# Modulation pieces in four column groups, and layer 0's first two pieces turned into columns on TensorE

## The chip, the cores and the metric

One Trainium2 chip, one core. The metric is the device time of one launch in microseconds (us), the median of several runs. TensorE multiplies (a stationary operand is loaded, a moving one streams past it), VectorE and ScalarE work element by element, GpSimd does the rest, SyncE issues most DMAs. All data are float32; each float32 matmul of the program is two records (two passes) in the trace, a transpose is one.

## The reference

Two layers of a transformer over 1024 tokens of an image and 256 of context, 1024 wide. Each layer is modulated: six vectors of 1024 numbers, for each of two conditions, are made from the conditions and shift, scale and gate what the layer does. Layer 0 mixes by retention and neighbourhood attention, layer 1 by windowed attention, and both go on with a mixture of 32 experts.

```python
s_c, s_cc = silu(c), silu(c_ctx)
for layer in range(2):
    sh1, sc1, g1, sh2, sc2, g2 = split((s_c @ ada_w[layer] + ada_b[layer])[:, None, :], 6)
    csh1, csc1, ... = split((s_cc @ ada_w[layer] + ada_b[layer])[None, None, :], 6)
    hx = rms_norm(x, norm_g[layer, 0]) * (1 + sc1) + sh1
    hc = rms_norm(xc, norm_g[layer, 0]) * (1 + csc1) + csh1
    ox, oc = mixer(hx, hc)
    x = x + g1 * ox;  xc = xc + cg1 * oc
    h2 = rms_norm(x, norm_g[layer, 1]) * (1 + sc2) + sh2
    x = x + g2 * moe(h2)          # likewise xc in layer 0
out = rms_norm(x, final_g)
```

ada_w is 2 x 1024 x 6144 in float32, 50 MB in all.

## The kernel before

The modulation is cut into 12 **pieces**: piece s is vector j = s % 6 of layer l = s // 6, 1024 columns of ada_w, for both conditions. Each piece has 4 MB of weights in two halves of 512 columns, loaded by `ada_load` (two DMAs of 2 MB) into one of two buffer pairs, and from piece 6 on into one pair alone (`ada_ring`), so that load s + 1 waits there for product s. `ada_product` multiplies on TensorE: the stationary operand is a 128 x 2 slice of the activated conditions (`sT`, one column for each condition), the moving one 512 columns of weights; half h writes partitions 32h and 32h + 1 of one PSUM bank, that is, column group h of the array, accumulating over eight slices k. `ada_evict` on VectorE adds the biases (which `ada_rows` has loaded into the row buffer `modrow[s % 2]`), and for the scale vectors (j of 1 and 4) computes (1 + scale) times the norm's gain. `ada_out` writes the two rows to the memory tensor `mod`. Later stages read gates and shifts from there as rows.

The first shift and scale of a layer (pieces 0, 1 and 6, 7) are wanted as columns, feature 8p + k of a vector in partition p: `ada_cols` reads them back from `mod` into `colab`. In layer 0 ScalarE issues these writes and reads (`ada_out(act, 0)`, `ada_out(act, 1)`, `ada_cols(act, 0)` in `n1_act`), in layer 1 SyncE.

The stage around them: `n1_act` and `n1_dve` compute each tile's root mean square and normalise it, `n1_pe` transposes it on TensorE (`turn`), and both engines evict the transposed tile to `hT` with `colab` as scale and bias. Behind that runs the projection `pa`: 40 **units**, each eight matmuls of 128 x 128 by 512 for one tile and one chunk of 512 columns of weights; before unit i, TensorE transposes tile i + 1, waits for tile i's eviction, and for odd i below 20 runs product 2 + i // 2. So TensorE's order is: products 0 and 1, transposes of tiles 0 and 1, unit 0, transposes of tile 2, product 2, unit 1, and so on until product 11. Products 0 and 1 run ahead of all, and their pieces are evicted between the scale computations of the decay (`ada_dve`) and after the normalising of tiles 0 and 1 (`n1_dve`).

SyncE's queue is written out by hand in `ada_sp`: loads of pieces 0 and 1 with their biases, three tiles of x, the first chunk of projection weights, then load 2, tiles, biases of piece 2, load 3, biases of piece 3, and so on. From piece 6 on the order is: write of piece s, biases of piece s + 2, load of piece s + 2. The biases of piece s + 2 go into the row buffer of piece s, so they wait until its write to memory has landed.

Semaphores are shared between names that follow one another: `share` maps a name to an earlier one, and `done` adds the earlier total.

## Time and profile before

| what | value |
| --- | --- |
| median of 3 runs | 2951.45 us (2949.23 to 2952.83) |
| profiled execution | 2954.52 us |
| its span, first to last instruction | 2952.4 us |
| TensorE matmul busy | 2734.9 us (93%), 11488 matmuls |
| VectorE busy | 1003.3 us (34%) |
| ScalarE busy | 594.2 us (20%) |
| GpSimd busy | 253.8 us (9%) |
| mean granted TensorE clock | 0.961 |
| moved by DMA | 602.72 MB, mean 204 GB/s |

The profile comes from one execution. Times in the trace count from the span's start. PE is TensorE's matmul side and PEld its weight loads, which overlap; DVE is VectorE, ACT ScalarE, SPq and ACTq the DMA issuing of SyncE and ScalarE. In a row of the timeline the first number is the start, the second the length of the merged group, and the brackets say how long the engine idled before it and what released it. Matmuls are pipelined, so that a record's length is not its price; the distance between starts is.

### The profile page before, as it was taken

Reading aid. Unit: us, or ns where it says so; the run is one execution under the profiler, and the core shown is the slowest. Engines: PE = TensorE matmul, PEld = TensorE weight load, DVE = VectorE, ACT = ScalarE, POOL = GpSimd, SP = SyncE. Lnnn points to the kernel's source line nnn. Section 1 sums busy time; section 2 is a strip of 40 time slices with the busy share of each in tenths; the row PEclk is TensorE's granted clock in tenths of the full one; section 3 lists DMA queues with packets and bytes.
Section 4 is the critical chain, followed back from the end, with each engine's and each line's share of the span. In section 5 each row is a group of like instructions: output and inputs, shape, how many; then the busy total and the mean of one; then the engine's idle time right before and its main releaser. Section 6 shows DMA issues by size and latency. Waiting matters only on the chain. (4 is left out here: it accounts for less than half of the span.)

```text
span 2952.4 us, 30072 instructions
## 1 busy us (share of the span) xinstructions
PE 2734.9 (93%) x11488; PEld 1401.9 (47%) x11488; DVE 1003.3 (34%) x2373; ACT 594.2 (20%) x1187; POOL 253.8 (9%) x359
## 2 busy tenths in 40 slices
PE   5999999999989799999999779989999799999991
PEld 1434446555745444444444334467765444444440
DVE  2221227306736621111111074267746511111113
ACT  2201101116821100000000041068831100000002
POOL 0011020003011100000000000000011100000003
PEclk8999999999999899999999989999999799999995
DMA  8654110205050289999999540030030599999994
GB/s 315 229 198 146 27 38 26 75 0 112 2 221 31 92 316 331 365 389 333 383 362 339 216 174 29 0 64 2 2 124 36 205 386 403 404 405 403 401 395 186
DMA packets 225944, 602.72 MB, mean 204 GB/s; under 512 B 18056, under 2 KB 21136, under 8 KB 217224
## 3 DMA queue, kind: packets, MB, share of 16 engines
q1 hardware_dynamic: 209976, 545.15, 51.2%
q0 software_dynamic: 15264, 55.58, 4.8%
q8 instruction: 94, 1.54, 0.2%
q14 instruction: 50, 0.41, 0.0%
q10 hardware_dynamic: 560, 0.03, 0.0%
HBM read 556.57 MB, written 44.42 MB: 204 GB/s over the span
## 5 line engine op out<-in xcount | busy, mean ns | idle before, releaser
L1688 PE MATMUL PS<-ar 128*128 128x512 f32 x2016 | 883.8, 596 | 3.4 <-DVE ar L1886 2.6
L778 PE MATMUL PS<-ar 128*128 128x512 f32 (+1 forms) x1600 | 678.5, 580 | 16.1 <-ACT ar L579 14.9
L1688 PEld LDWEIGHTS PS<-ar 128*128 128x128 f32 x2016 | 379.8, 191 | 475.4 <-issue 470.9
L778 PEld LDWEIGHTS PS<-ar 128*128 128x128 f32 x1600 | 300.3, 191 | 354.5 <-issue 334.9
L1308 PE MATMUL PS<-ar 128*128 128x512 f32 x576 | 255.9, 598 | 0.6 <-DVEq L331 0.6
L1691 PE MATMUL PS<-ar 128*64 128x512 f32 x1056 | 238.8, 605 | 15.4 <-DMA ar<-in_expert_w_gu_dram 13.7
L1182 DVE CUSTOM_DVE_ANT_0 ar<-PS,ar 128x640 f32<-128x640 f32 (+2 forms) x208 | 158.1, 797 | 204.7 <-POOL ar L1098 133.5
L1899 DVE COPY ar<-PS 128x512 f32<-128x512 f32 x53 | 36.7, 692 | 514.3 <-PE PS L1701 514.3
L1808 ACT ACTIVATE ar<-PS 128x512 f32<-128x512 f32 x53 | 31.7, 597 | 728.5 <-PE PS L1688 538.0
L1308 PEld LDWEIGHTS PS<-ar 128*128 128x128 f32 x576 | 107.6, 191 | 123.7 <-issue 122.9
L1237 ACT ACTIVATE ar<-ar 128x641 f32<-128x641 f32 (+4 forms) x208 | 159.5, 772 | 0.8 <-DVE ar L1182 0.8
L1691 PEld LDWEIGHTS PS<-ar 128*64 128x64 f32 x1056 | 77.6, 139 | 165.5 <-issue 163.4
L1226 ACT ACTIVATE ar<-PS 128x512 f32<-128x512 f32 (+1 forms) x208 | 133.6, 655 | 72.6 <-PE PS L1140 68.4
L1893 DVE TENSOR_TENSOR ar<-PS,ar 128x512 f32<-128x512 f32 x53 | 36.6, 691 | 323.7 <-PE PS L1688 239.6
L1128 PE MATMUL PS<-ar 64*128 64x256 f32 (+1 forms) x800 | 134.1, 453 | 11.7 <-DVE ar L1182 10.4
L1140 PE MATMUL PS<-cst,ar 128*128 128x128 f32 x944 | 128.5, 281 | 1.0 <-DVE ar L1192 0.8
L1151 PE MATMUL PS<-ar 128*64 128x128 f32 x1888 | 125.6, 278 | 0.0
L1140 PEld LDWEIGHTS PS<-cst,ar 128*128 128x128 f32 x944 | 102.6, 142 | 42.0 <-issue 34.7
L1962 POOL DMA_INDIRECT yd<-ar x53 | 51.8, 977 | 792.4 <-ACT ar L1814 417.6
L1814 ACT ACTIVATE ar<-PS 128x1024 f32<-128x1024 f32 x29 | 29.7, 1025 | 414.7 <-PE PS L1688 370.7
L1151 PEld LDWEIGHTS PS<-ar 128*64 128x64 f32 x1888 | 101.0, 136 | 17.2 <-issue 16.6
L489 PE MATMUL PS<-ar 128*2 128x512 f32 x384 | 89.3, 620 | 20.3 <-DMA ar<-in_ada_w_dram 20.3
(226 smaller groups left out, 1966.7 us busy)
## 6 DMA issues: line engine op xcount, KB each, us to landing
ar<-in_expert_w_gu_dram SPq DMA_DIRECT2D x128, 2048.0 KB, 17.7
ar<-in_expert_w_down_dram SPq DMA_DIRECT2D x64, 2048.0 KB, 17.3
ar<-in_ada_w_dram SPq DMA_DIRECT2D x24, 2048.0 KB, 13.5
ar<-yd SPq DMA_DIRECT2D x36, 512.0 KB, 6.7
ar<-in_ab_w_in_dram SPq DMA_DIRECT2D x7, 2048.0 KB, 9.0
h2d<-ar SPq DMA_DIRECT2D x18, 512.0 KB, 2.6
ar<-in_swa_w_in_dram SPq DMA_DIRECT2D x3, 2048.0 KB, 10.6
ar<-mod SPq DMA_DIRECT2D x3, 1536.0 KB, 8.0
```

The lines of the kernel that those rows point to most:

```text
L489: mm = nc.tensor.matmul(PS[32 * h:32 * h + 2, ada_bank(s), :], sT[:, k, :], adaw[q][h][:, k, :], start=(k == 0), stop=(k == KC - 1))
L778: mm = nc.tensor.matmul(out_, lhs, rhs, start=(k == 0), stop=(k == KC - 1))
L1128: mm = nc.tensor.matmul(score_cols(a, half, at, keys.shape[1]), u["q"][rows_], keys[rows_], start=True, stop=True)
L1140: tr = nc.tensor.transpose(turned_cols(to, P), xat[layer][2 * (i % 3) + a][:, c * P:c * P + P], ident)
L1151: mm = nc.tensor.matmul(slot_of(i)[64 * a:64 * a + 64], half["vs"][c], ptb[layer][i % 2][:, turned_at(a, half["n"]) + c * P:][:, 0:P], sta ...
L1182: nc.vector.tensor_tensor_reduce(out=xat[layer][b][:, 0:w], in0=score_cols(a, half, half["segs"][0][1], w), in1=half["bias"], scale=-SCALE ...
L1226: nc.scalar.activation(ptb[layer][i % 2][:, at:at + w], turned_cols(at, w), ACT.Copy).then_inc(S(f"{n}_pt"), 1)
L1237: nc.scalar.activation(x, x, ACT.Exp, bias=amx[:, b:b + 1], scale=-1.0, accum_out=sums[:, b:b + 1]).then_inc(S(f"{n}_e"), 1)
L1308: mm = nc.tensor.matmul(PS[:, 2 + half, :], mixed(i, k), WO[l][:, k, half * 512:half * 512 + 512], start=(k == 0), stop=(k == KC - 1))
L1688: return nc.tensor.matmul(out, lhsT, ws[0][:, k, cols], start=start, stop=stop)
L1691: mm = nc.tensor.matmul(out[half], lhsT[:, half], ws[h][:, k, cols], start=start, stop=stop)
L1962: pool.indirect_dma_start(out=yd, out_offset=bass.IndirectOffsetOnAxis(ap=dst_i[:, c:c + 1], axis=0), in_=yb[b % 2], in_offset=None).then_ ...
```

## The change

- A piece is multiplied in four column groups of 256 columns instead of two of 512: 32 matmuls for each piece instead of 16, in partitions 32c and 32c + 1 for c from 0 to 3. Row buffers have 256 columns in these partitions, and biases, gains and writes are strided over partitions accordingly, two DMAs for each as before (one for each condition).
- `ada_evict` has four instructions of 256 columns for each step instead of two of 512.
- Pieces 0 and 1 are no longer written to `mod` and read back. `ada_turn` on TensorE makes their columns: for each group c and each k, the stationary operand is 2 x 32 (every eighth number of the rows), the moving one 2 x 2 of the identity; the result is 32 partitions of two columns in bank 4 + s. Both turns stand behind product 1 and ahead of the transposes of tiles 0 and 1. Turn 0 waits for piece 0's eviction, turn 1 for the scaled rows of piece 1. `ada_columns` on VectorE copies them to `colab`.
- ScalarE issues none of these DMAs; it and VectorE wait for `cols0` before the first eviction in layer 0.
- The biases of pieces 2 and 3 wait for turns 0 and 1 instead of for writes.
- Three pairs of semaphores are shared that weren't.

```diff
--- before.py
+++ after.py
@@ -299,6 +299,9 @@
         for before, after in (("masks_in", "band_in1"), ("gain_in", "sink_in"), ("cos_in0", "cos_in1"), ("cos_in1", "fg_in")):
             share(("{}",), before, after, 16)
 
+        for before, after in (("dec_ln", "dec_pos"), ("dec_pos", "dec_exp"), ("silu_c", "rpb_scaled")):
+            share(("{}",), before, after, 1)
+
         chains = {}
 
         class Chain:
@@ -340,8 +343,8 @@
 
         ADA = 12
         adaw = [[R(a, 4096).rearrange("p (k n) -> p k n", k=KC) for a in pair] for pair in ((10240, 20480), (25600, 29696))]
-        modrow = [ar[0:34, a:a + 512] for a in (24576, 25088)]
-        ngrow = ar[0:34, 14400:14912]
+        modrow = [ar[:, a:a + 256] for a in (24576, 25088)]
+        ngrow = ar[:, 14400:14656]
         cin = R(14336, 16).rearrange("p (s k) -> p s k", s=2)
         sT = R(14352, 16).rearrange("p (k s) -> p k s", k=KC)
         rpbs = ar[0:NAH, 15360:15360 + 961].rearrange("p (c i) -> p c i", c=31)
@@ -371,35 +374,38 @@
                 sp.dma_start(adaw[q][h], A["ada_w"][l].rearrange("(p k) n -> p k n", k=KC)[:, :, c:c + 512])\
                     .then_inc(S(f"ada_in{q}"), 16)
 
+        def four(row):
+
+            return row.rearrange("(c n) -> c n", c=4)
+
         def ada_rows(sp, s):
 
             l, j = ada_of(s)
-            if s >= 2:
-                sp.wait_ge(*done(f"mod_out{s % 2}", 32 * (s // 2)))
-            for h in range(2):
-                sp.dma_start(modrow[s % 2][32 * h:32 * h + 2], A["ada_b"][l, j * D + h * 512:j * D + h * 512 + 512].partition_broadcast(2))\
-                    .then_inc(S(f"ada_b{s % 2}"), 16)
+            if s in (2, 3):
+                sp.wait_ge(*done("mod_tr", s - 1))
+            elif s > 3:
+                sp.wait_ge(*done(f"mod_out{s % 2}", 32 * (s // 2 - 1)))
+            for q in range(2):
+                sp.dma_start(modrow[s % 2][q:P:32], four(A["ada_b"][l, j * D:j * D + D])).then_inc(S(f"ada_b{s % 2}"), 16)
             if j in (1, 4):
                 if s > 1:
-                    sp.wait_ge(*done("mod_rows", 2 * (2 * l + j // 3)))
-                for h in range(2):
-                    sp.dma_start(ngrow[32 * h:32 * h + 2], A["norm_g"][l, j // 3, h * 512:h * 512 + 512].partition_broadcast(2))\
-                        .then_inc(S("ng_in"), 16)
+                    sp.wait_ge(*done("mod_rows", 4 * (2 * l + j // 3)))
+                for q in range(2):
+                    sp.dma_start(ngrow[q:P:32], four(A["norm_g"][l, j // 3])).then_inc(S("ng_in"), 16)
 
         def ada_out(eng, s):
             l, j = ada_of(s)
             if j in (1, 4):
-                eng.wait_ge(*done("mod_rows", 2 * (2 * l + j // 3 + 1)))
+                eng.wait_ge(*done("mod_rows", 4 * (2 * l + j // 3 + 1)))
             else:
-                eng.wait_ge(*done("ada_ev", 2 * (s + 1)))
-            for h in range(2):
-                c = j * D + h * 512
-                eng.dma_start(mod[l, :, c:c + 512], modrow[s % 2][32 * h:32 * h + 2]).then_inc(S(f"mod_out{s % 2}"), 16)
+                eng.wait_ge(*done("ada_ev", 4 * (s + 1)))
+            for q in range(2):
+                eng.dma_start(four(mod[l, q, j * D:j * D + D]), modrow[s % 2][q:P:32]).then_inc(S(f"mod_out{s % 2}"), 16)
 
         def ada_cols(eng, l):
 
             for q in range(2):
-                eng.wait_ge(*done(f"mod_out{q}", 32 * (3 * l + 1)))
+                eng.wait_ge(*done(f"mod_out{q}", 32 * 3))
             for s in range(2):
                 eng.dma_start(colab[:, l, s], mod[l, s, 0:2 * D].rearrange("(j p k) -> p j k", j=2, k=KC))\
                     .then_inc(S("cols_in"), 16)
@@ -483,30 +489,52 @@
             q = ada_ring(s)
             pe.wait_ge(*done(f"ada_in{q}", 32 * ada_fills(s)))
             if s >= 2:
-                pe.wait_ge(*done("ada_ev", 2 * (s - 1)))
+                pe.wait_ge(*done("ada_ev", 4 * (s - 1)))
             for k in range(KC):
-                for h in range(2):
-                    mm = nc.tensor.matmul(PS[32 * h:32 * h + 2, ada_bank(s), :], sT[:, k, :], adaw[q][h][:, k, :],
-                                          start=(k == 0), stop=(k == KC - 1))
+                for c in range(4):
+                    mm = nc.tensor.matmul(PS[32 * c:32 * c + 2, ada_bank(s), 0:256], sT[:, k, :],
+                                          adaw[q][c // 2][:, k, (c % 2) * 256:(c % 2) * 256 + 256], start=(k == 0), stop=(k == KC - 1))
             mm.then_inc(S("ada_mm"), 1)
+
+        def ada_turn(pe, s):
+
+            if s == 0:
+                pe.wait_ge(*done("consts", 32))
+                pe.wait_ge(*done("ada_ev", 4))
+            else:
+                pe.wait_ge(*done("mod_rows", 4))
+            for c in range(4):
+                at = slice(32 * c, 32 * c + 2)
+                for k in range(KC):
+                    tr = nc.tensor.matmul(PS[32 * c:32 * c + 32, 4 + s, 2 * k:2 * k + 2],
+                                          modrow[s][at].rearrange("s (p k) -> s k p", k=KC)[:, k, :], cst[at, C_ID + 32 * c:C_ID + 32 * c + 2],
+                                          start=True, stop=True)
+            tr.then_inc(S("mod_tr"), 1)
 
         def ada_pe(pe):
             pe.wait_ge(*done("silu_c", 1))
             for s in range(2):
                 ada_product(pe, s)
+            for s in range(2):
+                ada_turn(pe, s)
+
+        def ada_columns(dve, s):
+
+            dve.wait_ge(*done("mod_tr", s + 1))
+            nc.vector.tensor_copy(colab[:, 0, :, s, :], PS[:, 4 + s, 0:2 * KC].rearrange("p (k s) -> p s k", s=2)).then_inc(S("cols0"), 1)
 
         def ada_evict(dve, s):
             l, j = ada_of(s)
             dve.wait_ge(*done("ada_mm", s + 1))
             dve.wait_ge(*done(f"ada_b{s % 2}", 32 * (s // 2 + 1)))
-            half = [slice(32 * h, 32 * h + 2) for h in range(2)]
-            for p in half:
+            parts = [slice(32 * c, 32 * c + 2) for c in range(4)]
+            for p in parts:
                 m = modrow[s % 2][p]
-                nc.vector.tensor_tensor(m, PS[p, ada_bank(s), :], m, ALU.add).then_inc(S("ada_ev"), 1)
+                nc.vector.tensor_tensor(m, PS[p, ada_bank(s), 0:256], m, ALU.add).then_inc(S("ada_ev"), 1)
             if j in (1, 4):
-                dve.wait_ge(*done("ada_ev", 2 * (s + 1)))
+                dve.wait_ge(*done("ada_ev", 4 * (s + 1)))
                 dve.wait_ge(*done("ng_in", 32 * (2 * l + j // 3 + 1)))
-                for p in half:
+                for p in parts:
                     m = modrow[s % 2][p]
                     nc.vector.scalar_tensor_tensor(out=m, in0=m, scalar=1.0, in1=ngrow[p],
                                                    op0=ALU.add, op1=ALU.mult).then_inc(S("mod_rows"), 1)
@@ -596,10 +624,9 @@
             ahead(1)
             if l == 0:
                 act.wait_ge(*done("rpb_out", 16))
-                ada_out(act, 0)
-                ada_out(act, 1)
-                ada_cols(act, 0)
-            act.wait_ge(*done("cols_in", 32 * (l + 1)))
+                act.wait_ge(*done("cols0", 2))
+            else:
+                act.wait_ge(*done("cols_in", 32))
             evict(0)
 
             def before(i):
@@ -608,7 +635,7 @@
                     evict(i + 1)
                 if l == 0 and i == 2 * NT:
                     for q in range(2):
-                        act.wait_ge(*done(f"mod_out{q}", 16 * ADA))
+                        act.wait_ge(*done(f"mod_out{q}", 16 * (ADA - 2)))
             proj_act(act, (pa, pc)[l], before=before)
 
         def n1_dve(dve, l):
@@ -642,7 +669,11 @@
             ahead(1)
             if l == 0:
                 ada_evict(dve, 1)
-            dve.wait_ge(*done("cols_in", 32 * (l + 1)))
+                ada_columns(dve, 0)
+                ada_columns(dve, 1)
+                dve.wait_ge(*done("cols0", 2))
+            else:
+                dve.wait_ge(*done("cols_in", 32))
             evict(0)
 
             def before(i):
```

## Rows read from the trace of the kernel before

**Rows 1.** The page, part 2: TensorE's busy tenths in 40 slices.
```profile
PE   5999999999989799999999779989999799999991
```

**Rows 2.** Timeline of TensorE: start, length (us), instructions, idle before and its releaser.
```profile
29.47 9.58 PE L489 MATMUL PS<-ar 128*2 128x512 f32 x32 [3.89 <-DMA ar<-in_ada_w_dram]
38.98 2.06 PE L666 MATMUL PS<-cst,ar 128*128 128x128 f32 x16
55.98 10.08 PE L778 MATMUL PS<-ar 128*128 128x512 f32 x16 [14.94 <-ACT ar L579]
...
66.88 7.04 PE L489 MATMUL PS<-ar 128*2 128x512 f32 x32
73.85 7.13 PE L778 MATMUL PS<-ar 128*128 128x512 f32 x16
```

**Rows 3.** Timeline of all engines, from 34 to 56 us: VectorE and ScalarE.
```profile
34.09 1.38 DVE L505 TENSOR_TENSOR ar<-PS,ar 2x512 f32<-2x512 f32 x2
...
37.59 0.76 DVE L625 TENSOR_SCALAR ar<-ar,ssq 128x1024 f32<-128x1024 f32 x1
...
39.10 1.39 DVE L505 TENSOR_TENSOR ar<-PS,ar 2x512 f32<-2x512 f32 x2 [0.76 <-PE PS L489]
40.53 1.39 DVE L511 SCALAR_TENSOR_TENSOR ar<-ar 2x512 f32<-2x512 f32 x2
...
54.42 1.51 ACT L579 ACTIVATE ar<-PS,colab 128x128 f32<-128x128 f32 x4 [17.07 <-DMA colab<-mod]
```

**Rows 4.** Groups by line and shape, TensorE: count, busy us, mean ns, idle before.
```profile
L489 PE MATMUL PS<-ar 128*2 128x512 f32 x384 | 89.3, 620 | 20.3 <-DMA ar<-in_ada_w_dram 20.3
```

**Rows 5.** Waits of TensorE, whole span: us in total, times, longest.
```profile
PE PS L489 <- DMA ar<-in_ada_w_dram: 20.3, 3, 16.2
```

**Rows 6.** Timeline of weight loads (PEld) in attention, and in the router's product.
```profile
742.16 1.07 PEld L1151 LDWEIGHTS PS<-ar 128*64 128x64 f32 x20 [0.16 <-issue]
...
849.86 1.75 PEld L1327 LDWEIGHTS PS<-ar 128*128 128x128 f32 x15 [0.24 <-issue]
```

**Rows 7.** Groups by line and shape, VectorE, 0 to 330 us: an add of 256 columns.
```profile
L878 DVE TENSOR_TENSOR ar<-PS,ar 128x256 f32<-128x256 f32 x26 | 9.7, 415 | 0.0
```

**Rows 8.** Windows: busy us (count) of each engine, granted clock, DMA share, GB/s.
```profile
29.40:34.90 5.50, 5.43 (x14) 0.90 (x16) 1.28 (x3) 2.43 (x3) 0.00 (x0) 0.52 1.04 395
...
45.00:46.00 1.00, 0.00 (x0) 0.00 (x0) 0.00 (x0) 0.00 (x0) 0.00 (x0) 0.50 1.05 387
56.00:61.00 5.00, 5.00 (x6) 2.17 (x7) 2.35 (x7) 2.57 (x7) 0.00 (x0) 0.50 1.05 388
```

**Rows 9.** Timeline of SyncE's DMA issues around products 6 to 8.
```profile
163.72 1.26 SPq L371 DMA_DIRECT2D ar<-in_ada_w_dram  x2
...
171.35 2.83 SPq L397 DMA_DIRECT2D mod<-ar  x2
183.04 0.54 SPq L380 DMA_DIRECT2D ar<-in_ada_b_dram  x2
184.88 1.26 SPq L371 DMA_DIRECT2D ar<-in_ada_w_dram  x2
```

**Rows 10.** Timeline of TensorE around products 7 and 8.
```profile
177.81 7.03 PE L489 MATMUL PS<-ar 128*2 128x512 f32 x32 [0.20 <-DMA ar<-in_ada_w_dram]
...
192.27 1.09 PE L759 MATMUL PS<-ar 128*64 128x128 f32 x16
...
201.82 7.03 PE L489 MATMUL PS<-ar 128*2 128x512 f32 x32
```

**Rows 11.** Window behind load 8: the last two numbers are DMA share and GB/s.
```profile
198.00:200.00 2.00, 2.00 (x6) 0.90 (x5) 0.00 (x0) 0.00 (x0) 0.00 (x0) 1.00 0.04 13
```

**Rows 12.** Groups by line and shape: a small product that stands alone, matmul and load.
```profile
L1561 PE MATMUL PS<-ar,cst 128*64 128x16 f32 x2 | 0.3, 220 | 0.0
...
L1561 PEld LDWEIGHTS PS<-ar,cst 128*64 128x64 f32 x4 | 0.4, 134 | 1.5 <-issue 1.5
```

## The prediction

> **What bounds the kernel now.** I read the page first. TensorE is busy in nearly every slice of the span, at nine tenths from the second slice on; the first slice has five [rows 1]. So whatever shortens TensorE's own work after that slice should come off the span in full unless a transfer becomes late, and in the first slice the question is what TensorE waits for. Second, TensorE's timeline of the first 90 us [rows 2]: product 1 runs from 29.47, the transposes of the first tiles from 38.98 to 41.04, and then nothing until the first unit of the projection at 55.98. Third, the other engines there [rows 3]: VectorE finishes normalising tile 1 at 38.35, evicts piece 1 from 39.10 and scales it until 41.92; ScalarE then waits 17.07 us for the columns' way back from memory, and both engines first use them at 54.42. So the idle stretch is the way of pieces 0 and 1 to memory and back. Fourth, the other ten products: product 2 takes 66.88 to 73.85, and all twelve have the same shape (384 matmul records, 32 each) [rows 2, 4]. TensorE waits for their weights 20.3 us in all, in three waits [rows 5]: 16.2 at the very start, 3.9 before product 1, 0.2 before product 7. From product 2 on each product is TensorE time on the path.
>
> **The ten later products.** Now 16 matmuls of 512 columns, which run as 32 records in 7.04 us, 6.97 from start to the next unit's start. A 512 column pass alone costs 7.13/16 = 0.45 (a unit has 16 of them one behind the other) [rows 2]; 32 passes one by one would be 14.3 with that, so the two column groups already run side by side. After: 32 matmuls of 256 columns, 64 records, in four groups. If four groups run side by side as two do, the time is half: 3.5 us, a gain of 3.47 each, 34.7 in ten; I take 34.5 for the tail that a product keeps. The price of the case is the issue rate: 64 loads and 64 matmuls in 3.5 us is one pair per 55 ns. The trace has that rate: 20 loads, with a matmul behind each, in 1.07 us, 53.5 ns a pair, in two groups of 64 columns [rows 6]. So I take full overlap, and as bounds nothing (0) and 3.5 each. Four groups at once is not in the trace, and this is the largest uncertainty.
>
> The Trainium skill ("TensorE: Matmul & The Clock Gate", section "Measured speedup vs the span model") reports 2.38 times for three column groups, not 3; four at that efficiency would be 3.17 times, a product of 4.5 us by 14.3 us of passes, and the ten products would bring 25. The rows of two groups show about 2 times, so the trace disagrees for two and cannot say for four; part overlap is a rival below, with its price from rows. The same page (section "Back-to-back issue gap") has 62 ns for a matmul when hardware decode is off; by that a product would be 4.0 us and the ten would bring 30. The row with 53.5 ns speaks against it.
>
> **The front, layer 0's columns.** Removed: four writes and two reads through memory on ScalarE's queue. Added on TensorE: 32 tiny products (two records each) for piece 0 and as many for piece 1, ahead of the tile transposes; on VectorE, two small copies and eight more evictions of half the width. Step by step:
> - Evicting piece 0: 4 of 256 columns at 0.415 each [rows 7] = 1.66 instead of 1.38 [rows 3], so the work behind it is 0.28 late; tile 1's normalising ends at 38.63.
> - Product 1 still starts at 29.47, held by its weights. At the lower clock until 34.9 (0.52 granted) [rows 8], it should end at about 36. That is ahead of 38.63, so VectorE's chain and not the product is now last: the product's gain here is worth only the 0.7 us that VectorE waited.
> - Evicting piece 1 (1.66) and scaling it (1.66) with the hand-over: 42.0, no gain against 41.92.
> - Turning piece 0 runs on TensorE from 35.9, beside VectorE's work, and is hidden while it takes under 6 us. Piece 1 cannot begin before 42.1. 64 load and matmul pairs: 53.5 ns a pair is the fast row, and 1.75/15 = 117 ns the slow one (loads of 128 columns) [rows 6], so 3.4 to 7.5 us. The loads here have 32 columns, nearer to the fast row (64 columns); I take 64 ns, 4.1 us, to 46.2.
> - The tiles' transposes are queued behind that on TensorE: the first eight are half of 2.06 [rows 2], to 47.3. The copies of columns (under 0.2 each, on other data) go beside them. Then VectorE and ScalarE evict tile 0, from 54.42 to 55.98 in before, 1.56: unit 0 starts at 48.9 instead of 55.98. **Gain 7.1**, with 3.7 and 7.8 at the two prices of a pair.
> - Unit 0 took 10.08 instead of 7.13 [rows 2] because the granted clock was 0.50 (1.2 GHz) until 61 [rows 8]; TensorE had idled from 41, with the clock down by 45 [rows 8]. After the change TensorE has work at 36 to 40, 42 to 47 and from 49, so the clock may stay up, which would give 3.0 more; or the tiny products, which stream two columns each, may keep it no busier than idling does. I take cold, and keep the 3.0 for the low end.
>
> **What transfers do.** The next bound is the ring of one pair of buffers from product 6 on: a load of 4 MB starts when the product before has ended. Product 6 ended and load 7 went out at 163.72; product 7 started at 177.81 after its 0.2 wait [rows 9, 10]. The units between are untouched, so that stays. For load 8 SyncE must first have passed the bias rows (183.04), which wait for the write of piece 6, issued 171.35 [rows 9], behind load 7 in the queues. In before that was done before product 7's end at 184.8; counted from load 7's issue it is at +19.9, and product 7 will now end at +17.6. Load 8 therefore starts 2.3 us after it could. It took 13.3 (184.88 until the transfers had gone quiet by 198.2) [rows 9, 11], and product 8 was wanted 17.0 after product 7's end (201.82 against 184.84) [rows 10]: 2.3 + 13.3 = 15.6, so 1.4 us are left. The cover is thin: were the load to take 3 us longer, it costs 1.6 us. I put it at nothing. SyncE's bias rows for pieces 2 and 3 now wait for the turned pieces (about 40 and 46) instead of for the writes (43.69 and later), so no load of weights goes out later; the queue behind them is no worse. Row writes and reads have four descriptors instead of two, of 1 KB, below what the trace lets me price; product 2 comes at 60, the loads for it were issued at 34.5.
>
> On VectorE each later piece costs two or four more instructions, 0.3 to 0.6 us, while a unit of 7 us runs on TensorE; without that cover it would be some 4 us in ten (the estimate of 0.28 for each row of four, from the first eviction above).
>
> **The sum.** 34.5 + 7.1 = 41.6 us. The profiled execution took 2954.5 us, its span 2952.4, so 2912.9 and 2910.8 in its terms; the median of the runs is 2951.45, 3.1 below the profiled execution, and gives **2909.9 us**. After this stage everything is started by the stages' own work, TensorE being busy, so the gain should be kept to the end.
>
> **The rivals.**
> - Four groups overlap only in part (an issue or read limit between two and four streams). The price of a pair is then that of the short burst: 16 narrow matmuls in 1.09 us, 68 ns [rows 10]. 64 of them are 4.35 us, a gain of 2.65 each, 26.5, and with the front 33.6: 2917.8. For it: no row has four groups, and the longest burst of narrow pairs in the rows has 20; against it: two groups lose nothing.
> - No more than two groups at once: 7 us a product as now. Only the front is left: 2944.4. The same time comes out if the tiny products do not pipeline on their tile, and each costs a load and a matmul in series, 134 + 220 ns [rows 12]: 64 of them are 22.7 us, twice, unit 0 at about 83, and 34.5 less 27.5 is a gain of 7. Against it: loads of 15 matmuls on one tile follow at 117 ns [rows 6].
> - **Slower:** the four groups run one after the other, for example because a bank written by four groups at once, or the read of four streams, is served in turn. 64 passes of 256 columns at 0.21 are 13.7 us, 6.7 more in each of ten; less the front's 7: 3011. It decides as soon as a product takes over 7.7 us. Against it: two groups in one bank overlap now.
>
> **How the numbers follow.** Full overlap 0.72 (of it 0.3 with unit 0 warm, 2906.9); part 0.15; 2944 in its two forms 0.10; slower 0.03. The range takes in a warm unit 0 with tiny products at the fast row and, above, part overlap with tiny products at the slow row: 2903 to 2921, which leaves out 0.13. A measurement of this kernel tells 0.2%, 5.9 us, from no change. 2944 is 7 us below, so half of that case's 0.10 counts as same: faster 0.92, same 0.05, slower 0.03.
>
> **What would show it.** Products 2 to 11: 64 records in about 3.6 us each; 4.35 or 7 would be the rivals. Unit 0 near 49, the tiny products of piece 1 from about 42 in about 4 us. Wait before product 7 at 0.2 and none before product 8. The stretches between products should be as before, and the gain at the end of the projection stage should equal the gain of the span; if it is less, a transfer or a later stage took it back.

## The result and the profile after

| | before | after |
| --- | --- | --- |
| median | 2951.95 us (2949.23 to 2952.83, 4 runs) | 2910.38 us (2909.01 to 2912.83, 4 runs) |
| ratio after / before | | 0.9856, 95% interval 0.9843 to 0.9868 |
| profiled execution | 2954.52 us | 2912.83 us |
| its span | 2952.4 us | 2910.7 us |
| TensorE matmul busy | 2734.9 us | 2699.1 us |
| TensorE matmuls | 11488 | 12000 |

The change makes the kernel faster by 41.6 us between the medians; the interval of the ratio is 39 to 46 us. The forecast was 2909.9, from 34.5 for ten products and 7.1 for the front. The traces show where it came from. First TensorE's timeline of the changed kernel (start, length, instructions, and idle before with its releaser), to be read against [rows 2]. L495 is a product, L509 a turn (the tiny products that turn a piece's rows into columns), L697 the transposes of a tile, L809 a unit:

```profile
28.49 6.26 PE L495 MATMUL PS<-ar 128*2 128x256 f32 x64 [6.84 <-DMA ar<-in_ada_w_dram]
34.81 3.41 PE L509 MATMUL PS<-cst,ar 2*32 2x2 f32 x64
41.18 3.44 PE L509 MATMUL PS<-cst,ar 2*32 2x2 f32 x64 [2.96 <-DVE ar L539]
44.55 3.38 PE L697 MATMUL PS<-cst,ar 128*128 128x128 f32 x16
48.21 7.13 PE L809 MATMUL PS<-ar 128*128 128x512 f32 x16 [0.27 <-ACT ar L607]
55.18 1.05 PE L697 MATMUL PS<-cst,ar 128*128 128x128 f32 x8
56.16 3.64 PE L495 MATMUL PS<-ar 128*2 128x256 f32 x64
59.73 7.13 PE L809 MATMUL PS<-ar 128*128 128x512 f32 x16
```

Product 2 takes 3.57 us (56.16 to 59.73) where it took 6.97, so 3.40 less, and all ten are alike: 34.0. Unit 0 starts at 48.21 instead of 55.98, 7.8 sooner, and product 2 at 56.16 instead of 66.88, 10.7 sooner, because unit 0 itself runs in 7.13 instead of 10.08.

The front on VectorE, against [rows 3] (timeline of the changed kernel). From the landing of the table of relative biases (first line) to piece 1's scaled rows (41.13) VectorE works with no idle gap over 0.3 us:

```profile
32.39 0.58 DVE L579 TENSOR_SCALAR ar<-ar 8x465 f32<-8x465 f32 x1 [3.61 <-DMA ar<-in_na_rpb_dram]
32.90 1.77 DVE L533 TENSOR_TENSOR ar<-PS,ar 2x256 f32<-2x256 f32 x4
...
37.56 1.78 DVE L533 TENSOR_TENSOR ar<-PS,ar 2x256 f32<-2x256 f32 x4
39.37 1.76 DVE L539 SCALAR_TENSOR_TENSOR ar<-ar 2x256 f32<-2x256 f32 x4
...
46.64 1.37 DVE L658 TENSOR_SCALAR ar<-PS,colab 128x128 f32<-128x128 f32 x4 [1.80 <-PE PS L697]
```

Around products 7 and 8 (TensorE's timeline, then SyncE's issues), against [rows 9, 10]:

```profile
149.90 3.63 PE L495 MATMUL PS<-ar 128*2 128x256 f32 x64
153.46 7.13 PE L809 MATMUL PS<-ar 128*128 128x512 f32 x16
...
171.31 3.64 PE L495 MATMUL PS<-ar 128*2 128x256 f32 x64 [0.74 <-DMA ar<-in_ada_w_dram]
```

```profile
155.40 1.10 SPq L389 DMA_DIRECT2D ar<-in_ada_b_dram  x2
156.55 1.29 SPq L374 DMA_DIRECT2D ar<-in_ada_w_dram  x2
157.88 4.54 SPq L403 DMA_DIRECT2D mod<-ar  x2
```

Product 7 ends at 153.46 and its buffers are free, but load 8 goes out at 156.55, behind the biases of piece 8: 3.1 us late. Product 8 starts 14.76 us after that, at 171.31, and has waited 0.74.

Put side by side, the two traces show the gain growing by 3.4 with each product to 44.1 us at the end of the projection stage (its last transposes start at 326.50 instead of 370.61), and it is still 44.9 us where the last expert stage begins (2324.87 instead of 2369.75). At the end of the span it is 41.7. So 3 us are missing again in the last stage, and the landing so near the forecast has two parts: a front that gained 3.6 more than forecast (10.7 instead of 7.1), and a last stage that seems to give most of it back. That was the first question to settle.

### The profile page after: what moved, and what is told of

Its sections match the earlier page's. It is cut to its first block and busy times, and to the rows that moved or that the text cites. A ratio compares the mean times of both kernels' runs of the same rounds, so it can differ in the third digit from the quotient of the medians.

```text
span 2910.7 us, 31123 instructions
## 1 busy us (share of the span) xinstructions
PE 2699.1 (93%) x12000; PEld 1410.7 (48%) x12000; DVE 1010.8 (35%) x2407; ACT 594.2 (20%) x1187; POOL 254.9 (9%) x359
## 5 line engine op out<-in xcount | busy, mean ns | idle before, releaser
L809 PE MATMUL PS<-ar 128*128 128x512 f32 (+1 forms) x1600 | 675.2, 578 | 1.4 <-issue 1.1
L809 PEld LDWEIGHTS PS<-ar 128*128 128x128 f32 x1600 | 299.1, 190 | 333.4 <-issue 328.5
L1722 PE MATMUL PS<-ar 128*64 128x512 f32 x1056 | 239.8, 607 | 17.5 <-DMA ar<-in_expert_w_gu_dram 16.0
L1722 PEld LDWEIGHTS PS<-ar 128*64 128x64 f32 x1056 | 77.6, 139 | 168.6 <-issue 166.5
L1159 PE MATMUL PS<-ar 64*128 64x256 f32 (+1 forms) x800 | 134.3, 454 | 11.3 <-DVE ar L1213 10.1
L1171 PEld LDWEIGHTS PS<-cst,ar 128*128 128x128 f32 x944 | 102.3, 142 | 42.5 <-issue 32.9
L1223 DVE TENSOR_SCALAR ar<-ar 128x640 f32<-128x640 f32 (+2 forms) x208 | 105.6, 550 | 3.7
```

The source lines that it names most:

```text
L809: mm = nc.tensor.matmul(out_, lhs, rhs, start=(k == 0), stop=(k == KC - 1))
L1159: mm = nc.tensor.matmul(score_cols(a, half, at, keys.shape[1]), u["q"][rows_], keys[rows_], start=True, stop=True)
L1171: tr = nc.tensor.transpose(turned_cols(to, P), xat[layer][2 * (i % 3) + a][:, c * P:c * P + P], ident)
L1223: nc.vector.tensor_scalar(x, x, sums[:, b + a:b + a + 1], None, ALU.mult).then_inc(S(f"{n}_n"), 1)
L1722: mm = nc.tensor.matmul(out[half], lhsT[:, half], ws[h][:, k, cols], start=start, stop=stop)
```

## The experiments

All ratios are to the kernel before on the same chip. Times inside a run are from its trace. Of the longer edits only the main lines are shown, with "..." between them.

**Is the last stage longer because of the change?** It is the expert stage in which TensorE waits for weights. The next rows are windows over it, of before and after (busy time and count of each engine, then granted clock, DMA share and GB/s):

```profile
2400.00:2900.00 500.00, 473.35 (x1603) 204.96 (x1601) 80.98 (x85) 11.95 (x21) 38.94 (x41) 0.98 0.99 386
```

```profile
2355.00:2860.00 505.00, 474.45 (x1604) 205.03 (x1602) 81.09 (x85) 12.06 (x21) 39.07 (x41) 0.98 0.99 384
```

Both windows reach past the stage's last matmul and hold the same work, 474 us of TensorE's time, with the DMA engines 99% busy and 2 GB/s apart. The window of the first expert stage in the changed kernel shows that a high DMA share alone does not mark a stage as paced by transfers:

```profile
1163.00:1598.00 435.00, 435.00 (x1312) 200.02 (x1312) 51.46 (x59) 32.45 (x40) 36.98 (x38) 1.00 1.00 364
```

There the share is 1.00 as well, but TensorE is busy in all of the 435 us and waits for nothing. Both kernels were then run again, unedited.

> The kernel before once more, for a second trace. Theory A (the last expert stage varies by itself): its length differs by 1 to 4 us from that in the first trace of this kernel, and everything up to it repeats within 0.5 us. Theory B (it is fixed, and the change lengthens it): it repeats within 0.5 us.

> The changed kernel once more, for a second trace. Theory A (what its first trace gives back after the projection stage, 44.1 us there against 41.7 at the end, comes from the last expert stage, which is paced by the transfers of expert weights and varies by itself): the span up to the last expert stage repeats within 0.5 us and that stage differs by 1 to 4 us between the two traces. Theory B (the change itself makes that stage longer, for instance by another phase of the transfers): it repeats within 0.5 us, at about 2.5 more than in the kernel before.

> The changed kernel a third time, beside the reordered one on the same chip. Theory: its ratio to the kernel before is 0.985 as before; unit 0 starts at 48 to 50, and takes 7.1 to 8.6 by where the clock rises; the last expert stage is 512 to 515 us long.

The length of the stage, from its first to its last group of matmuls with 64 columns of weights (L1691 in before, L1722 in after), is 511.9 and 512.5 us in the two traces of the kernel before, and 515.0, 514.0 and 512.3 in three of the changed one; in the other seven whole traces below it runs from 510.8 (load_first) to 514.7 (order_both), and four of the five that hold the change's main part and its later stages (narrow128, order_pe, load_first, all_orders) lie at 510.8 to 512.4. TensorE's waits for expert weights (us in total, times, longest) go the same way in the main. The first traces of before and of after:

```profile
PE PS L1691 <- DMA ar<-in_expert_w_gu_dram: 13.7, 6, 3.1
```

```profile
PE PS L1722 <- DMA ar<-in_expert_w_gu_dram: 16.0, 8, 3.1
```

The other trace of before has 13.4 us, the other two of after 15.4 and 13.1, and load_first, with the shortest stage, 12.6.

The expectation of theory A was too wide for the kernel before (0.6 apart, not 1 to 4), and the part before the last stage repeats less well than the 0.5 us I had written (2367.54 and 2369.75 at its start in before, 2324.87, 2329.51 and 2324.09 after). But theory B, a stage lengthened by some 2.5 us by the change, falls: the third trace of the same kernel and four variants of it, at 510.8 to 512.4, are no longer than the kernel before. A lengthening of about 1 us stays open: the mean over the eight traces with the whole change is 512.9 us, over the two of before 512.2. Timed, after_again is 2908.89 us against 2952.89 (0.9846, 0.9830 to 0.9863) and after_third 2909.29 against 2954.1 (0.9853, 0.9837 to 0.9870), 44 and 45 us: what the projection stage gained is the gain of the whole within these intervals. The 3 us were the scatter of one profiled execution in a stage that waits for its transfers.

**Do the two parts add up?**

> The change with its second part undone: four column groups, layer 0's columns through memory again. Theory (the two parts add up): a product takes 3.57 us from start to the next unit's start, as in the changed kernel, so ten bring 34.0; unit 0 starts near 56 as in the kernel before, cold, because the way through memory sets it; no wait of over 1 us before product 8. Gain at the end of the projection stage 33 to 34.5, of the whole 31 to 35 (2917 to 2921). Rival (the shorter products need the earlier start, or the transfers in the ring eat them when the front is late): gain under 28.

```diff
-            for s in range(2):
-                ada_turn(pe, s)
...
+                ada_out(act, 0)
+                ada_out(act, 1)
+                ada_cols(act, 0)
+            act.wait_ge(*done("cols_in", 32 * (l + 1)))
```

2918.57 us against 2952.89, ratio 0.9882 (0.9866 to 0.9899), 34.8 us by the ratio. Unit 0 starts at 56.31 and takes 9.98, as in before:

```profile
28.86 6.53 PE L493 MATMUL PS<-ar 128*2 128x256 f32 x64 [6.77 <-DMA ar<-in_ada_w_dram]
...
56.31 9.98 PE L802 MATMUL PS<-ar 128*128 128x512 f32 x16 [17.65 <-ACT ar L603]
...
67.11 3.63 PE L493 MATMUL PS<-ar 128*2 128x256 f32 x64
```

Its gain at the end of the projection stage is 33.8 us (336.83 against 370.61). Product 1, which ends before 36 now instead of 39, brings nothing: VectorE still scales piece 1 until 41.1 (41.9 in before), the reads of the columns go out at 46.94 instead of 46.56, and the columns are first used at 54.75 instead of 54.42.

> The change with its first part undone: two column groups of 512, layer 0's columns by tiny products (32 record pairs for each piece, since each takes 64 columns of the result). Theory: a pair costs 53 ns whatever the width of its load up to 64 columns and whatever the clock, so a turn takes 1.7 us; product 1 ends at 39, its rows are ready at 41.9, turned by 43.7; unit 0 starts at 46.5 to 47.5, and runs in 7.13 if the clock has risen by then, in up to 10 if not. Gain at the end of the projection stage 8.5 to 12.5, all of it before product 2; products stay at 6.97. Rival (tiny products run one behind the other): a turn takes 11 us and nothing is gained.

```diff
-                for c in range(4):
-                    mm = nc.tensor.matmul(PS[32 * c:32 * c + 2, ada_bank(s), 0:256], sT[:, k, :],
...
+                for h in range(2):
+                    mm = nc.tensor.matmul(PS[32 * h:32 * h + 2, ada_bank(s), :], sT[:, k, :], adaw[q][h][:, k, :],
...
-                    tr = nc.tensor.matmul(PS[32 * c:32 * c + 32, 4 + s, 2 * k:2 * k + 2],
+                    tr = nc.tensor.matmul(PS[64 * c:64 * c + 64, 4 + s, 2 * k:2 * k + 2],
```

2943.88 us, ratio 0.9971 (0.9960 to 0.9983), 8.6 us; at the end of the projection stage 10.0 (360.57 against 370.61). Added to 34.8 that is 43.4, and the whole change has 42.5 to 45.5 by its three ratios. In the traces, which tell it more sharply, 33.8 and 10.0 are 43.8 at the end of the projection stage, where the whole change has 44.1. The parts add up. But a step of my expectation was wrong:

```profile
37.97 6.54 PE L509 MATMUL PS<-cst,ar 2*64 2x2 f32 x64
44.44 3.68 PE L697 MATMUL PS<-cst,ar 128*128 128x128 f32 x16
48.09 7.92 PE L809 MATMUL PS<-ar 128*128 128x512 f32 x16
```

A pair is a weight load and its matmul. A turn has 32 pairs here and I gave it 1.7 us; the two took 6.5, 3.3 each, nearly as long as with 64 pairs of half the width (3.4). A pair costs 53 ns at 32 columns and 102 at 64: not a fee for issuing, but the time of the load. Yet the attention's loads of 64 columns take 53.5 [rows 6]. What sets the turns apart is that they read every eighth number of a row, and from two rows instead of 128.

**Is it the stride?**

> The changed kernel with turns that read 32 adjacent numbers of a row as stationary operand instead of every eighth, so that layer 0's shift and scale columns hold the features in another order (the right order is left out; the routing and so the expert stages change with it, and only the first 60 us are to be read). Theory (a pair in a turn is bound by its load, and a load of every eighth number costs double): a turn takes 1.7 to 1.9 us instead of 3.4, 27 ns a pair, and unit 0 starts 1.5 us sooner after piece 1's rows. Rival (the double price comes from loads of two rows or from the 32 x 32 tile, not from the stride): 3.4 us as before.

```diff
-                                          modrow[s][at].rearrange("s (p k) -> s k p", k=KC)[:, k, :], cst[at, C_ID + 32 * c:C_ID + 32 * c + 2],
+                                          modrow[s][at].rearrange("s (k p) -> s k p", k=KC)[:, k, :], cst[at, C_ID + 32 * c:C_ID + 32 * c + 2],
```

```profile
36.09 1.88 PE L509 MATMUL PS<-cst,ar 2*32 2x2 f32 x64
42.28 3.01 PE L509 MATMUL PS<-cst,ar 2*32 2x2 f32 x64 [4.30 <-DVE ar L539]
```

Turn 0 takes 1.88 us instead of 3.41, 29 ns a pair instead of 53: the stride nearly doubles the load, as the theory said. Turn 1 is only 0.4 shorter. It runs at the lower clock (0.50 granted from 39 to 48), turn 0 at the higher (1.00 at 36 and 37). So a pair with adjacent numbers costs 46 ns at the lower clock (2.94 us for 64, from start to the transposes' start), while the strided one costs 53 at either clock. Unit 0 starts 0.4 sooner after piece 1's rows, not 1.5 as expected.

**What bounds a product now?** In my sum the issue rate of 53.5 ns a pair stood just under the 55 that four groups need.

> The changed kernel, with the later ten products cut once more: 64 matmuls of 128 columns in four groups, 128 pairs of a load and a matmul where it has 64. The streaming time of the array is the same. Theory (a product is bound by the columns that stream through four groups at once, and issuing a pair with a load of two columns is cheaper than 27 ns): 3.6 to 3.8 us from start to the next unit. Rival (a product of the changed kernel already stands at a floor of some 53 ns for each pair): 6.8 to 7.0 us, and the gain of the groups is gone: span 33 us longer than the changed kernel's.

```diff
+            n = 256 if s < 2 else 128
+            for e, k, c in itertools.product(range(256 // n), range(KC), range(4)):
+                at = (c % 2) * 256 + n * e
+                mm = nc.tensor.matmul(PS[32 * c:32 * c + 2, ada_bank(s), n * e:n * e + n], sT[:, k, :],
+                                      adaw[q][c // 2][:, k, at:at + n], start=(k == 0), stop=(k == KC - 1))
```

```profile
58.98 3.67 PE L496 MATMUL PS<-ar 128*2 128x128 f32 x128
62.58 7.13 PE L810 MATMUL PS<-ar 128*128 128x512 f32 x16
```

128 pairs in 3.60 us, 28 ns each, and 2911.48 us in its one run. So a product is bound by the columns that stream, not by issuing, and the rival with a floor of 53 ns falls. What the 53.5 ns row [rows 6] was is only argued: by a unit's rate (6.97 us for 16 passes of 512 columns) a pass of 128 columns takes 109 ns, so two groups give one each 54 ns; a load of 64 adjacent columns, estimated at up to 58 ns (twice the 29 of turn_contig), would fit as well.

**What brings the clock back before unit 0?**

> The changed kernel with turn 1 cut to one of its 32 tiny products, and the scale columns taken from turn 0's (so the scale of layer 0's first modulation is left out). Theory (turn 1 is on the path with its whole length, 3.4 us, and the clock in unit 0 depends on what TensorE did in the 6 us before): unit 0 starts 3.4 us sooner, 44.8 to 45.7, but the clock is still low in it, so it takes 9 to 10 us and product 2 starts less than 1 us sooner than in the changed kernel. Rival (tiny products do nothing for the clock, the transposes alone bring it back): unit 0 sees the higher clock from some 3 us after the transposes start, takes 7.1 to 7.5, and product 2 starts 3 us sooner.

```diff
-            for c in range(4):
+            for c in range(4) if s == 0 else (3,):
...
-                for k in range(KC):
+                for k in range(KC) if s == 0 else (0,):
...
-            nc.vector.tensor_copy(colab[:, 0, :, s, :], PS[:, 4 + s, 0:2 * KC].rearrange("p (k s) -> p s k", s=2)).then_inc(S("cols0"), 1)
+            nc.vector.tensor_copy(colab[:, 0, :, s, :], PS[:, 4, 0:2 * KC].rearrange("p (k s) -> p s k", s=2)).then_inc(S("cols0"), 1)
```

```profile
41.26 0.28 PE L509 MATMUL PS<-cst,ar 2*32 2x2 f32 x2 [2.96 <-DVE ar L539]
41.47 3.67 PE L697 MATMUL PS<-cst,ar 128*128 128x128 f32 x16
45.12 7.24 PE L809 MATMUL PS<-ar 128*128 128x512 f32 x16
...
53.17 3.63 PE L495 MATMUL PS<-ar 128*2 128x256 f32 x64
```

Only its first 60 us are to be read. Unit 0 starts 3.1 sooner than in the changed kernel and still takes 7.24, so product 2 is 3.0 sooner. The rival is right: the clock comes back without the tiny products of turn 1. Its windows (the granted clock is the third number from the end):

```profile
44.00:45.00 1.00, 1.00 (x6) 0.74 (x4) 0.91 (x3) 1.00 (x5) 0.00 (x0) 0.50 1.05 387
45.00:46.00 1.00, 1.00 (x3) 0.59 (x3) 0.00 (x0) 1.00 (x3) 0.00 (x0) 0.81 1.05 387
46.00:47.00 1.00, 1.00 (x3) 0.38 (x2) 0.56 (x3) 0.78 (x5) 0.00 (x0) 1.00 1.06 391
```

Here it rises just after unit 0's start at 45.12. In the first trace of the changed kernel it rises before unit 0 starts at 48.21, so unit 0 cannot be what raised it:

```profile
47.00:48.00 1.00, 0.94 (x6) 0.74 (x4) 1.00 (x4) 1.00 (x4) 0.00 (x0) 0.75 1.05 401
```

In the one trace turn 1 is all but missing, in the other unit 0 has not begun; what both have is the transposes. And turn 0 of the changed kernel does not hold the clock: TensorE is busy throughout 37 to 38, and the clock falls in it, some 2.5 us after product 1's end:

```profile
36.00:37.00 1.00, 1.00 (x23) 1.00 (x22) 0.61 (x4) 0.33 (x3) 0.00 (x0) 1.00 1.04 394
37.00:38.00 1.00, 1.00 (x23) 1.00 (x22) 0.94 (x2) 0.00 (x0) 0.00 (x0) 0.63 1.05 397
38.00:39.00 1.00, 0.22 (x4) 0.14 (x3) 0.93 (x3) 0.00 (x0) 0.00 (x0) 0.50 1.05 385
```

In turns_only, where both turns run without a gap from 37.97 to 44.44, it falls shortly before 43, in the middle of them:

```profile
42.00:43.00 1.00, 1.00 (x14) 1.00 (x13) 0.00 (x0) 0.00 (x0) 0.00 (x0) 0.94 1.10 408
43.00:44.00 1.00, 1.00 (x11) 1.00 (x10) 0.00 (x0) 0.00 (x0) 0.00 (x0) 0.50 1.01 379
```

The Trainium skill ("TensorE: Matmul & The Clock Gate", section "Part 4: PE-mode transpose") says that transposes do not engage the higher clock. These traces disagree, for float32: in turn1_one the clock rose within the first half microsecond of unit 0, with nothing but transposes and one tiny product since 41.3, and in the changed kernel it rose ahead of unit 0. When it rises is not the same each time: 3 to 6 us after the transposes' start. Unit 0 took 7.13, 7.29 and 8.09 us in three traces of the changed kernel, and 8.26 and 7.97 in narrow128 and load_first, which are the same up to there.

**Is there more in the front?** Two orders, the second with the first in it.

> The changed kernel with the transposes of tile 0 ahead of turn 1 on TensorE, where it idles for 3 us waiting for piece 1's scaled rows. Theory (the path from piece 1's rows to unit 0 is turn 1, then the first eight transposes, then the eviction): tile 0's transposes leave the path, unit 0 starts 2.0 us sooner, 46.2 to 47.1, if its clock then is as high as now it is worth 2.0, if low it loses 3. Rival (the eviction waits for something else, such as the copies on VectorE): under 0.5 us sooner.

```diff
-            for s in range(2):
-                ada_turn(pe, s)
+            ada_turn(pe, 0)
...
             turn(0)
+            if l == 0:
+                ada_turn(pe, 1)
```

> As the one before, and VectorE evicts and scales piece 1 ahead of normalising tile 1. Theory: piece 1's rows are ready 1.4 us sooner, so with the transposes off the path unit 0 starts 3.4 us sooner than in the changed kernel, 44.8 to 45.8; the clock in it decides whether product 2 is 3.4 us sooner or none, and the weights of product 2, whose load was issued at 33 and takes up to 19 us, are wanted at 53 and may be late by up to 1 us. Ratio to the kernel before 0.983 to 0.985. Rival (product 1's end at 34.8 to 36 or the transfers set the start): under 1 us sooner.

```diff
             ahead(0)
-            ahead(1)
             if l == 0:
                 ada_evict(dve, 1)
+            ahead(1)
+            if l == 0:
                 ada_columns(dve, 0)
```

From the first eviction on VectorE to unit 0 it is 15.3 us in the changed kernel, 13.6 in order_pe and 12.5 in order_both (46.63 less 34.17), so 1.7 and 2.9 of the expected 2.0 and 3.4. The start itself was within the expected range in order_pe (47.06) and 0.8 late in order_both (46.63), because the chain on VectorE starts when the table of relative biases lands, and that moved between 32.2 and 34.1 us by itself. Unit 0 took 8.55 and 8.04 us; the second is within what it took in the usual order (7.13 to 8.26), so that an earlier start brings a longer unit 0 is not shown. Counted from the first eviction to product 2 it is 22.9 and 21.3 us, against 23.3 to 24.4 in five traces of the usual order (three of the changed kernel, narrow128, load_first). So order_both brings 2 to 3 us there, and the totals, 2911.68 us in one run for order_pe and 2909.11, ratio 0.9845 (0.9828 to 0.9861), for order_both, are too wide to tell it.

> The changed kernel with SyncE issuing load s + 2 ahead of the biases of piece s + 2, from piece 6 on. Theory (load 8 goes out 3 us after product 7 has ended, because it stands behind the wait for the write of piece 6): load 8 goes out within 0.2 us of product 7's end, and the wait of 0.3 to 0.7 before product 8 is gone; biases land behind 4 MB of weights, 13 us later, which nobody needs sooner. 0.5 us in the trace, nothing that the time can show. Rival (the biases' later landing holds VectorE's eviction and product 10 or 11 waits for it): a wait of over 1 us before a later product.

```diff
                 if s + 2 < ADA:
-                    ada_rows(sp, s + 2)
                     ada_load(sp, s + 2)
+                    ada_rows(sp, s + 2)
```

Load 8 goes out at 154.87, as product 7 (151.18 to 154.8) ends, and there is no wait before product 8 or later; since after_third has none before product 8 either, it is the time of the issue that shows the effect. Product 7 waited 0.44. One run gave 2906.88 us; half a microsecond of that can be the edit.

> The changed kernel with the transposes of tile 0 between the turns, piece 1's eviction ahead of tile 1's normalising, piece 0's eviction no longer behind the wait for the table of relative biases, and loads ahead of biases. Theory (the front is VectorE's chain from the landing of that table, 32.4 to 34.1 in the traces so far; without it product 1's end at 35 to 36 is last): piece 1's rows are ready at 38.5 to 39.7, unit 0 starts at 43.6 to 45, product 2 at 52 to 54, where its weights may make it wait; gain over the changed kernel 3 to 5 us, ratio to the kernel before 0.983 to 0.9845. Rival (the transfers, busy without a gap until 62, hold product 2 at 55): at most 1 us over the changed kernel.

```diff
-            dve.wait_ge(*done("rpb_in", 16))
-            nc.vector.tensor_scalar(rpbs[:, :, 8:23], rpbi, 1.0 / SCALE, None, ALU.mult).then_inc(S("rpb_scaled"), 1)
             ada_evict(dve, 0)
...
             ahead(0)
             if l == 0:
+                dve.wait_ge(*done("rpb_in", 16))
+                nc.vector.tensor_scalar(rpbs[:, :, 8:23], rpbi, 1.0 / SCALE, None, ALU.mult).then_inc(S("rpb_scaled"), 1)
                 ada_evict(dve, 1)
```

```profile
28.75 1.77 DVE L532 TENSOR_TENSOR ar<-PS,ar 2x256 f32<-2x256 f32 x4
...
33.44 0.58 DVE L668 TENSOR_SCALAR ar<-ar 8x465 f32<-8x465 f32 x1
35.18 1.77 DVE L532 TENSOR_TENSOR ar<-PS,ar 2x256 f32<-2x256 f32 x4 [1.17 <-PE PS L495]
36.99 1.76 DVE L538 SCALAR_TENSOR_TENSOR ar<-ar 2x256 f32<-2x256 f32 x4
```

```profile
35.03 3.44 PE L509 MATMUL PS<-cst,ar 2*32 2x2 f32 x64
38.41 1.97 PE L697 MATMUL PS<-cst,ar 128*128 128x128 f32 x8
40.31 3.44 PE L509 MATMUL PS<-cst,ar 2*32 2x2 f32 x64
43.68 1.97 PE L697 MATMUL PS<-cst,ar 128*128 128x128 f32 x8
45.61 8.34 PE L811 MATMUL PS<-ar 128*128 128x512 f32 x16
...
54.77 3.63 PE L495 MATMUL PS<-ar 128*2 128x256 f32 x64
```

Now product 1 is last on the way to piece 1's rows, as expected: VectorE waits 1.17 for it, and the rows are ready at 38.75. But turn 1 starts only at 40.31, because TensorE is still at turn 0 and the first eight transposes: from product 1's end at 35.03 to unit 0 at 45.61 TensorE works without a gap, so turn 0, which was hidden before, is now on the path. That costs 1.6 us. The second eight transposes ahead of unit 0 run at the lower clock as well, 1.97 where they were 1.04 at the higher. So unit 0 starts at 45.61, later than my 43.6 to 45. Product 2 starts at 54.77, against 56.16 to 57.18 in the changed kernel's three traces, and its weights are there: no wait. 2908.72 us, ratio 0.9851 (0.9835 to 0.9868), beside 0.9853 (0.9837 to 0.9870) for the changed kernel in the same comparison: 1.4 to 2.4 us at product 2 in the traces, not told apart in the time. The rival's bound, at most 1 us, held for the total, its reason (the transfers hold product 2) did not.

## Why the prediction was right, point by point

- **What bounds the kernel:** right. Work taken from TensorE after the first slice came off one for one, and was kept through both attention and expert stages within the scatter of the traces (the start of the last expert stage moved by 5.4 us between traces of the changed kernel).
- **Ten products, 34.5:** measured 34.0. Full overlap of four groups held (3.57 us, 3.40 each; the forecast was 3.47 with 0.2 off in all). The fear about the issue rate rested on a row that I took for a rate of issue; narrow128 gives 28 ns a pair. Part overlap and the slower rival fall with every trace.
- **The front, 7.1:** unit 0 started 7.8 sooner in the first pair of traces, and product 2 10.7. By its terms: the tiny products of piece 1 took 3.4, not 4.1 (0.7 more gain), the table of relative biases happened to land 1.2 sooner than in before, which brought piece 1's rows 0.9 sooner than forecast (the evictions took 1.77, not 1.66), the eight transposes ran at the lower clock, 2.0 instead of 1.0 (1.0 less). So part of this gain was luck. VectorE's chain and not product 1 was last, as forecast. The cover of turn 0 held (34.81 to 38.2, rows of piece 1 at 41.1).
- **Unit 0 cold, the 3.0 kept for the low end:** this was the wrong choice of the two. The clock rose before unit 0 or within its first 3 us in every trace with turns, saving 1.5 to 3.0 of the 10.1. The forecast had priced this case, at 3.0. My argument for warm (tiny products are work) was not the cause either; the transposes, which now end just ahead of unit 0 instead of 15 us before it, are.
- **The price of a pair at 64 ns:** the value was near (53), the reason was not. It is the strided load; the choice "nearer to the fast row by its width" was luck, as a width of 64 columns costs 102 ns here.
- **The ring at product 8, nothing with 1.4 us of slack:** off by 2.1. Product 8 waited 0.74, 0.40 and 0 in the three traces. Two terms of the sum were too small. Load 8 went out 3.1 instead of 2.3 late, as I had put no price on the row DMAs: the two issues of the biases took 1.10 instead of 0.54 with rows that stride over four partitions. And I gave the load 13.3, up to where the transfers fall quiet (a row that shows this only to 2 us); product 8 could start 14.8, 14.4 and at most 13.9 us after the issue. The rows had a better number: in before, product 7 started 14.1 us after load 7's issue, after a wait [rows 9, 10].
- **The sum, 41.6:** measured 41.6 in the first comparison, 44 and 45 in the later ones. By the terms above the change is worth 44 at the end of the projection stage (34.0 for the products, 10.7 for the front with the warm unit 0, less 0.5 for the waits in the ring). So the hit of 2909.9, half a microsecond from the first median, owes something to chance; the range of 2903 to 2921 holds all three medians.

## What to carry to other kernels

A product with a tiny stationary side (two columns here) is bound by how many columns stream one behind the other; spread over all four column groups it took 3.57 us, a quarter of the serial time (an estimate: 64 passes of 256 columns at a unit's rate are 13.9 us), and halving the matmuls' width again cost nothing (3.60). A few numbers that must change from rows to columns are cheaper turned on TensorE than sent through memory where the engine idles anyway, but read the stationary operand with adjacent elements if the layout allows. When the front of a kernel is shortened, look at the granted clock of the first dense work after it: unit 0 took 10.1 us at the lower clock and 7.1 at the higher, and by when the clock rose it moved by 1.1 us between traces of the same instructions. Before a stage is called bound by its transfers, look at what TensorE waits for there, not at the DMA share alone.

## What the runs showed of the hardware that I had not expected

- A weight load of every eighth float32 number from two rows cost nearly twice that of adjacent ones: 53 ns for 32 columns, against 29 for the whole pair with adjacent numbers at the higher clock and 46 at the lower; 102 ns for 64 columns, against 53.5 for attention's pairs. The strided price is the same at both clocks (turn 0 3.41 us, turn 1 3.44).
- A pair of a two column load and a matmul can follow the last one in 28 ns (128 pairs in 3.60 us).
- Turns of tiny products, with TensorE busy all the time by its records, did not keep the higher clock (it fell between 37 and 38 us in the changed kernel, before 43 in turns_only); with 16 float32 transposes behind them it rose ahead of unit 0 (47 to 48 us in the changed kernel).
- The last expert stage, in which TensorE waited 12.5 to 16.0 us for weights (99% DMA share), varied by 4 us in 512 between traces of kernels that do the same in it, while the first, with as high a share (100%) but no wait, measured 435.31 or 435.32 us in each of twelve traces.
